# Making the dt columns of a hybrid block by position: 32 weight columns move past tiles of x

## The chip, the cores and the metric

The kernel runs on one core of one Trainium2 chip. The metric is the device time of one execution in microseconds (us), the median of several runs.

## The reference, cut to what matters

A hybrid block works on 256 positions of 2048 channels: a mixer (SSD scan and short convolution), cross attention, a SwiGLU layer, and then a second block of another kind. All is float32. This case is about 32 of the input projection's columns, `dt_raw`, and what is made of them for the scan:

```python
proj = h @ w_in                                   # h: rmsnorm(x), 256 x 2048
z, xbc, dt_raw, sc_u, sc_b, sc_c = jnp.split(proj, IN_SPLITS, axis=-1)   # dt_raw: 256 x 32
dt = jax.nn.softplus(dt_raw + dt_bias)            # 32 heads
a = -jnp.exp(a_log)
...
x = xh * dt[..., None]
a_cs = jnp.cumsum(dt * a, axis=position)          # running sum over the 256 positions
decay = jnp.exp(where(causal, a_cs[..., :, None] - a_cs[..., None, :], -inf))
```

So the scan needs, for each head, dt by position (a column per head, positions on the partitions), and the running sum a_cs in both forms: as rows (heads on the partitions, positions along them) and as columns.

## The kernel before, in words

**Split products.** A float32 product is made of three products in the fp32r format, which TensorE takes in one pass: every weight tile is split into a high part (`wh`, ScalarE, line 1209) and a low part (`wl`, VectorE, line 1556), every activation tile lies in SBUF as 256 high columns and 256 low columns side by side. A tile of 128 x 128 weights is then two matmuls: the high weights stand and 512 columns move past them (line 974), and the low weights stand and 256 columns move (line 971). The result has channels on the partitions. Every matmul has its own weight load (LDWEIGHTS, the rows named PEld).

**Units.** Weights come in units of 512 KB (1024 words in each partition). There are 902 units, in a list built by `columns()`. A unit is loaded by SP (`load`, line 826) into one of four `raw` buffers, split into one of four `wh`/`wl` buffers, and used by TensorE in list order. `schedule()` is an order written out by hand: each step s holds unit s of TensorE and pieces of work for the other engines (`PLAN[s]`); every engine walks through the steps in order and does its own pieces. The split of unit s+3 is a piece of step s, so weights are split three units ahead. The split of unit u on ScalarE waits until TensorE is through unit u-4, and SP's load of unit u waits for the split of unit u-4.

**The dt column.** It comes after `b` 1, as units 24 and 25: `w_dt` is the 32 columns padded with zeros to 128, so that the 16 tiles of 128 x 128 take two units of eight tiles, all into bank 0 (`ONE`, line 964), 32 of 128 output partitions in use. Unit 26 begins the column `u` 2, and `c` 2 is the next to write bank 0. Pieces `dt0` to `dt6` follow at 2, 7, 8, 12, 14, 18 and 19 steps behind unit 25:

- dt0: ScalarE copies the low half of the sum out of PSUM, VectorE adds the high half, multiplies with the norm's factor (a row, 32 partitions) and adds dt_bias.
- dt1 to dt4: softplus by |x|, exp, ln and a correction step (a reciprocal among it), and then dt*a, on tiles of 32 partitions x 256; the last instruction is the running sum (`tensor_tensor_scan`, line 1793).
- dt5: TensorE turns a_cs and dt into columns, four transposes of 32 x 128 (line 988), and dt6 copies them to `dcol`.
- acsw (16 steps behind): SP writes a_cs to a DRAM scratch, from where it is later broadcast.

**Order of the matmuls.** `unit_orders()` picks, unit by unit, whether 512 and 256 columns alternate (EVEN), come in groups (HEAD), or alternate in twos (TWOS), by where other TensorE work (the set `OTHER`) breaks in.

Of the kernel before, what the change touches and what calls it, by code (L numbers as in the profile page):

```python
# [13 lines left out]
NW = 4  # L14
# [7 lines left out]
    ("hy_b", 18), ("hy_skip", 6), ("norm_ffn_2", 16), ("fc_w", 264), ("fc_b", 88),  # L22
    ("dt_bias", 1), ("a_log", 1), ("f_b1", 1), ("f_fr1", 1), ("f_b2", 1),
    ("f_fr2", 1), ("rcnt", 64),
# [46 lines left out]
def columns():  # L71
# [161 lines left out]
def schedule():  # L233
# [49 lines left out]
    for c in COLS:  # L283
# [197 lines left out]
    for step in at:  # L481
# [4 lines left out]

ONE = [(k, 0, m) for k in range(8) for m in range(2)]
# [4 lines left out]
OTHER = {"nmm", "nmm2", "ntr", "ntr2", "snt", "bmm", "dt5", "cbm", "ssd0", "ssd3", "sn0", "fz1m", "fz2m", "fhm", "fkm", "ztm", "zfm", "zim",  # L492
         "gmm", "pool1", "att0", "att3", "att5", "htr"}


def unit_orders():


    broken = {s + 1: {piece for piece, i in PLAN[s]} & OTHER for s in STEPS if s >= 0}
    starts = sorted({0, *(s for s, other in broken.items() if other and s < NU),  # L500
                     *(u for u in range(1, NU) if UNITS[u - 1][0].src in ("w_o", "w_down_2", "w_gv1") and
                       UNITS[u][0].src != UNITS[u - 1][0].src)})
# [21 lines left out]
def program(nc, T_):  # L524
# [38 lines left out]
    d_part = [sem(f"d_part{i}") for i in range(4)]  # L563
    d_par0, d_par, d_ident, d_mask, d_f1, d_f2, d_b2 = (sem("d_" + n) for n in ("par0", "par", "ident", "mask", "f1", "f2", "b2"))
    d_out = [sem(f"d_out{i}") for i in range(3)]
# [105 lines left out]
    mask = a_(9728, 384)  # L671
    dtb = [a_(10112 + 256 * i, 256, 32) for i in range(8)]
    acs = dtb[7]
    dcol = a_(12160, 128)
# [221 lines left out]
    def tensor(e):  # L896
# [5 lines left out]
        def unit(u, tiles=range(8), halves_=(0, 1)):  # L902
# [3 lines left out]
            elif u == c.first and c.before:  # L906
# [5 lines left out]
                elif p.kind == "dt":  # L912
                    w.wait_ge(dtV, 1)
                elif p.kind in ("r", "rn"):
# [7 lines left out]
            if u > 1:  # L922
                w.wait_ge(lo, halves(u))
            st, sp = u == c.first, u == c.last
            if c.kind == "v" or c.src == "w_gv1":
                for kk in range(c.kn):
# [35 lines left out]
            else:  # L962
                order = ONE if c.w == 128 else ORDER[u]
                for kk, i, low in order:
                    X, kx, s, n = xtile(c, g * c.kn + kk)
# [24 lines left out]
        for s in STEPS:  # L990
# [15 lines left out]
            for piece, i in PLAN[s]:  # L1006
# [52 lines left out]
                if piece == "dt5":  # L1059
                    w.wait_ge(d_ident, 16)  # L1060
                    w.wait_ge(dtV, 13)
                    for n, src in enumerate((acs, dtb[4])):
                        for st in range(2):
                            o = 64 * n + 32 * st
                            t = turn(banks[7][:, o:o + 32], src[:, 128 * st:128 * st + 128], p=32)
                    t.then_inc(dtP, 1)
                if piece == "cbm":
                    b = banks[4 + i]
                    w.wait_ge(xbc, 4 + i + 1)
                    w.wait_ge(br, 6 * 7 + 1)  # L1070
                    w.wait_ge(dtA, 6)
                    w.wait_ge(nrs, 2)
# [132 lines left out]
    def scalar(e):  # L1205
# [10 lines left out]
        for s in STEPS:  # L1216
            for piece, i in PLAN[s]:
# [3 lines left out]
                if piece == "split":  # L1221
                    r, b = i % NRAW, i % NW
                    w.wait_ge(d_raw[r], 16 * (i // NRAW + (r > 0)))
                    if i >= NW:
                        w.wait_ge(mm, i - NW + 1)
                    copy(wh[:, b * UN:(b + 1) * UN], raw[:, r * UN:(r + 1) * UN]).then_inc(hi, 1)
                if piece == "mgain":
# [160 lines left out]
                if piece == "dt0":  # L1388
                    w.wait_ge(mm, i.last + 1)
                    copy(dtb[1], bank(i, 0)[0:32, 256:512]).then_inc(dtA, 1)  # L1390
                if piece == "dt1":
                    w.wait_ge(dtV, 3)
                    e.activation(dtb[1], dtb[0], ACT.Abs).then_inc(dtA, 1)
                    w.wait_ge(dtA, 2)
                    e.activation(dtb[1], dtb[1], ACT.Exp, scale=-1.0).then_inc(dtA, 1)
                    e.activation(dtb[5][:, 0:1], P("a_log", p=32), ACT.Exp).then_inc(dtA, 1)
# [3 lines left out]
                if piece == "dt6":  # L1400
                    w.wait_ge(dtP, 1)
                    copy(dcol, banks[7][:, 0:128]).then_inc(dtA, 1)
                if piece == "silu":
# [16 lines left out]
                if piece == "ssd1":  # L1420
                    q = i % 2
                    w.wait_ge(d_bb[i % 3], 16 * (i // 3 + 1))
                    w.wait_ge(dtA, 6)
                    if i > 1:
                        w.wait_ge(sMg, i - 1)
                        w.wait_ge(sMv, i - 1)
                    else:
                        w.wait_ge(dtP, 1)
                        w.wait_ge(bsl, 16)
# [122 lines left out]
    def vector(e):  # L1552
# [11 lines left out]
        for s in STEPS:  # L1564
            for piece, i in PLAN[s]:
# [4 lines left out]
                if piece == "split":  # L1570
                    r, b = i % NRAW, i % NW
                    w.wait_ge(hi, halves(i))
                    tt(wl[:, b * UN:(b + 1) * UN], raw[:, r * UN:(r + 1) * UN], wh[:, b * UN:(b + 1) * UN].bitcast(F32),
                       ALU.subtract).then_inc(lo, 1)
# [186 lines left out]
                if piece == "dt0":  # L1761
                    x = dtb[0]
                    w.wait_ge(dtA, 1)
                    tt(x, bank(i, 0)[0:32, 0:256], dtb[1], ALU.add).then_inc(dtV, 1)
                    w.wait_ge(nrs, 1)
                    w.wait_ge(dtV, 1)
                    tt(x, x, rsb(0)[0:32, :], ALU.mult).then_inc(dtV, 1)
                    w.wait_ge(dtV, 2)
                    ts(x, x, P("dt_bias", p=32), None, ALU.add).then_inc(dtV, 1)
                if piece == "dt2":  # L1770
                    w.wait_ge(dtA, 3)
                    ts(dtb[2], dtb[1], 1.0, None, ALU.add).then_inc(dtV, 1)
# [9 lines left out]
                if piece == "dt4":  # L1782
                    b2, b3, b4 = dtb[2], dtb[3], dtb[4]
                    w.wait_ge(dtA, 5)
# [3 lines left out]
                    stt(b4, dtb[0], 0.0, b4, ALU.max, ALU.add).then_inc(dtV, 1)  # L1788
                    w.wait_ge(dtV, 10)
                    ts(b2, b4, dtb[5][:, 0:1], -1.0, ALU.mult, ALU.mult).then_inc(dtV, 1)  # L1790
                    e.memset(b3, 1.0).then_inc(dtV, 1)
# [6 lines left out]
                if piece == "ssd1":  # L1798
                    q = i % 2
                    w.wait_ge(sT, i + 1)  # L1800
                    w.wait_ge(dtA, 6)
                    if i > 1:
                        w.wait_ge(sY, i - 1)
                    else:
                        w.wait_ge(cb, 4)
                        w.wait_ge(dtP, 1)
                    for st in range(2):
# [497 lines left out]
```

## Time and profile before

| | us |
|---|---|
| median of 3 runs | 2587.53 (2586.18 to 2587.93) |
| the profiled execution, first to last instruction (span) | 2585.8 |
| TensorE matmul busy | 2576.9 |
| TensorE weight load busy | 2245.3 |
| VectorE busy | 1893.6 |
| ScalarE busy | 1469.0 |
| GpSimd busy | 316.3 |

The page gives the profiled execution's span and no device time of its own; the median of the runs lies 1.7 us above that span. Busy times overlap: a weight load runs beside the matmul before it. In the rows, PE is TensorE's matmuls, PEld its weight loads, DVE VectorE, ACT ScalarE, POOL GpSimd, and L974 is line 974 of the kernel.

### The profile page before, as it was taken

The page shows a single profiled execution, that of the slowest core. Times are in us where ns is not written, and L with a number is a line of the kernel's source. Part 1 is how long each engine was busy: PE and PEld are TensorE (multiplying, and loading weights), DVE is VectorE, ACT ScalarE, POOL GpSimd, SP SyncE. Part 2 cuts the span into 40 slices and gives each one's busy share as a digit, 9 for nine tenths or more (in the row PEclk, how much of TensorE's full clock was granted, in tenths as well). Part 3 has the DMA queues.
Part 4 walks back from the last instruction along what each step waited for, and adds up shares of the span by engine and source line. Part 5 has one row for each costly group of instructions (what it writes and reads, how often), then busy time and mean ns, then how long its engine had stood idle before and what let it go on. Part 6 is the DMA issues. An engine that isn't in the chain of part 4 may idle for free.

```text
span 2585.8 us, 37666 instructions
## 1 busy us (share of the span) xinstructions
PE 2576.9 (100%) x14704; PEld 2245.3 (87%) x14704; DVE 1893.6 (73%) x2859; ACT 1469.0 (57%) x2244; POOL 316.3 (12%) x292
## 2 busy tenths in 40 slices
PE   9999999999999999999999999999999999999998
PEld 8888888888899888888888888888888888888887
DVE  7787777777977866666666698788876766667675
ACT  6666657776656444444444466445654545555554
POOL 2111103316201010101000043101100000000000
PEclk9999999999999999999999999999999999999999
DMA  7665666666656656666666666556666666666665
GB/s 245 181 221 186 188 200 199 175 207 189 211 172 197 182 173 189 190 192 187 192 189 190 192 184 224 157 171 189 187 198 192 190 193 189 194 189 194 188 190 159
DMA packets 137065, 493.73 MB, mean 191 GB/s; under 512 B 15415, under 2 KB 15800, under 8 KB 136504
## 3 DMA queue, kind: packets, MB, share of 16 engines
q1 hardware_dynamic: 136456, 490.80, 62.7%
q8 instruction: 116, 1.90, 0.3%
q14 instruction: 61, 0.50, 0.1%
q10 hardware_dynamic: 432, 0.53, 0.1%
HBM read 489.14 MB, written 2.13 MB: 190 GB/s over the span
## 4 chain that ended last, share of the span: by engine, by line
PE 99%; DMA 0%; ACT 0%; DVE 0%; issue 0%; SPq 0%; ACTq 0%
PE ps L974 56%; PE ps L971 28%; PE ps L947 3%; PE ps L946 3%; PE ps L948 3%; PE ps L935 0%; PE ps L936 0%; PE ps L934 0%; PE ps L988 0%; PE ps L1097 0%; PE ps L960 0%; PE ps L959 0%; PE ps L961 0%; PE ps L1184 0%; PE ps L1173 0%; PE ps L1153 0%
## 5 line engine op out<-in xcount | busy, mean ns | idle before, releaser
L974 PE MATMUL ps<-X,wh 128*128 128x512 f32 x4752 | 1591.1, 395 | 1.1 <-DVE X L1562 1.1
L1556 DVE TENSOR_TENSOR wl<-raw,wh 128x1024 fp32r<-128x1024 f32 (+1 forms) x908 | 1149.7, 1269 | 511.8 <-ACT wh L1209 511.1
L1209 ACT ACTIVATE wh<-raw 128x1024 fp32r<-128x1024 f32 (+1 forms) x908 | 955.4, 1055 | 730.8 <-PE ps L971 555.1
L971 PE MATMUL ps<-X,wl 128*128 128x256 f32 x4752 | 1199.0, 278 | 0.0
L974 PEld LDWEIGHTS ps<-X,wh 128*128 128x128 f32 x4752 | 862.8, 188 | 171.9 <-issue 3.0
L971 PEld LDWEIGHTS ps<-X,wl 128*128 128x128 f32 x4752 | 872.0, 188 | 37.9
L974 PE MATMUL ps<-XG,wh 128*128 128x512 f32 x1472 | 492.0, 394 | 0.0
L971 PE MATMUL ps<-XG,wl 128*128 128x256 f32 x1472 | 371.6, 278 | 0.0
L974 PEld LDWEIGHTS ps<-XG,wh 128*128 128x128 f32 x1472 | 266.8, 188 | 53.1 <-issue 0.9
L1209 ACT ACTIVATE T<-ps 128x256 f32<-128x256 f32 x444 | 145.7, 380 | 251.5 <-PE ps L971 249.7
L971 PEld LDWEIGHTS ps<-XG,wl 128*128 128x128 f32 x1472 | 269.7, 188 | 11.3
L2108 POOL TENSOR_TENSOR hT<-hT,T 128x256 f32<-128x256 f32 x144 | 123.3, 877 | 820.1 <-DVE hT L1556 820.0
L1556 DVE TENSOR_TENSOR hT<-hT,ps 128x256 f32<-128x256 f32 (+1 forms) x280 | 109.3, 437 | 52.5 <-ACT T L1209 44.4
L946 PE MATMUL ps<-wh,XG 128*128 128x512 f32 x352 | 137.0, 389 | 0.0
L947 PE MATMUL ps<-wl,XG 128*128 128x512 f32 x352 | 136.9, 389 | 0.0
L948 PE MATMUL ps<-wh,XG 128*128 128x512 f32 x352 | 136.9, 389 | 0.0
L1562 DVE SCALAR_TENSOR_TENSOR T<-R,par,T 128x256 f32<-128x256 f32 x260 | 109.0, 482 | 0.8 <-ACT T L1366 0.8
L2108 POOL TENSOR_TENSOR T<-T 128x512 f32<-128x512 f32 (+1 forms) x54 | 71.4, 1326 | 231.2 <-ACT T L1267 216.8
L1556 DVE TENSOR_TENSOR T<-ps,T 128x256 f32<-128x256 f32 x130 | 49.0, 418 | 48.7 <-ACT T L1209 48.6
L1556 DVE TENSOR_TENSOR R<-ps,T 128x256 f32<-128x256 f32 x130 | 49.0, 419 | 48.3 <-ACT T L1209 48.3
L946 PEld LDWEIGHTS ps<-wh,XG 128*128 128x128 f32 x352 | 66.1, 188 | 13.8
L948 PEld LDWEIGHTS ps<-wh,XG 128*128 128x128 f32 x352 | 66.1, 188 | 13.7
(228 smaller groups left out, 1629.6 us busy)
## 6 DMA issues: line engine op xcount, KB each, us to landing
raw<-in_w_gate SPq DMA_DIRECT2D x176, 512.0 KB, 3.7
raw<-in_w_down SPq DMA_DIRECT2D x176, 512.0 KB, 3.7
raw<-in_w_sc SPq DMA_DIRECT2D x95, 512.0 KB, 4.1
raw<-in_w_up SPq DMA_DIRECT2D x88, 512.0 KB, 3.8
raw<-in_w_val SPq DMA_DIRECT2D x88, 512.0 KB, 3.6
raw<-in_w_zx SPq DMA_DIRECT2D x80, 512.0 KB, 4.1
raw<-in_w_in SPq DMA_DIRECT2D x56, 512.0 KB, 3.9
raw<-in_w_osc SPq DMA_DIRECT2D x32, 512.0 KB, 3.7
```

What stands on the lines that cost most here:

```text
L946: e.matmul(bank(c, i)[:, :], xh, wh[:, b0:b0 + 512], start=not goes and st and kk == 0, stop=False)
L947: e.matmul(bank(c, i)[:, :], xh, wl[:, b0:b0 + 512], start=False, stop=False)
L948: t = e.matmul(bank(c, i)[:, :], xl, wh[:, b0:b0 + 512], start=False, stop=sp and kk == c.kn - 1 and (not goes or c.kind == "on"))
L971: t = e.matmul(bank(c, i)[:, 0:256], wl[:, b0:b0 + 128], X[:, kx * 512:kx * 512 + 256], start=False, stop=sp and kk == c.kn - 1)
L974: e.matmul(bank(c, i)[:, :], wh[:, b0:b0 + 128], X[:, kx * 512:kx * 512 + 512], start=st and kk == 0, stop=False)
L1209: return e.activation(out, in_, ACT.Copy, scale=scale)
L1556: return e.tensor_tensor(out, a, b, op)
L1562: return e.scalar_tensor_tensor(out, a, s1, b, op0, op1)
L2108: return e.tensor_tensor(out, a, b, op)
```

## The change

`w_dt` is no longer padded: 32 columns x 16 tiles are one unit of 256 KB, so there are 901 units. The roles in the matmul are swapped. The activation tiles stand and the weights move: for each of 16 channel tiles and each of the two halves of the positions, the high activations (128 channels x 128 positions) stand while 64 columns move (32 high weights, 32 low weights side by side), and then the low activations stand while the 32 high weights move. The result has positions on the partitions: 128 x 64 in each of banks 0 and 1. Softplus and dt*a then run on tiles of 128 x 64, dt lands in `dcol` directly, and dt_bias and a_log come by a DMA that broadcasts 128 values to all partitions. dt*a is turned into rows (dt5, two transposes of 128 x 32), the running sum is made from PSUM (dt6), and a_cs is turned back into columns (dt7, two transposes of 32 x 128) and copied (dt8). The pieces stand at 1, 3, 4, 5, 7, 18, 20, 30 and 31 steps behind the dt unit, acsw at 21.

```diff
-            add("dt", 0, "w_dt", 0, range(2), "1", 0, w=128, kn=8)
+            add("dt", 0, "w_dt", 0, range(1), "1", 0, w=32, kn=16)
...
-            for n, d in enumerate((2, 7, 8, 12, 14, 18, 19)):
+            for n, d in enumerate((1, 3, 4, 5, 7, 18, 20, 30, 31)):
                 put(e + d, "dt%d" % n, c)
-            put(e + 16, "acsw", 0)
+            put(e + 21, "acsw", 0)
...
+    def by_tile(t, b):
+        return t[:, b * UN:b * UN + 1024].rearrange("p (k m) -> p k m", k=16)
...
-            e.dma_start(raw[:, r * UN:(r + 1) * UN], T_[col.src][col.c, g]).then_inc(d_raw[r], 16)
+            n = col.w * col.kn
+            e.dma_start(raw[:, r * UN:r * UN + n], T_[col.src][col.c, g]).then_inc(d_raw[r], 16)
...
+                        e.dma_start(dtp, T_["dtp"].to_broadcast([128, 128])).then_inc(d_dtp, 16)
...
+            if c.kind == "dt":
+                both = by_tile(wh, u % NW)
+                for kk in range(16):
+                    X, kx, s, n = xtile(c, kk)
+                    w.wait_ge(s, n)
+                    for i in range(2):
+                        xh, xl = (X[:, kx * 512 + o + 128 * i:kx * 512 + o + 128 * i + 128] for o in (0, 256))
+                        e.matmul(bank(c, i)[:, 0:64], xh, both[:, kk, :], start=kk == 0, stop=False)
+                        t = e.matmul(bank(c, i)[:, 0:32], xl, both[:, kk, 0:32], start=False, stop=kk == 15)
+                t.then_inc(mm, 1)
+                return
...
                 if piece == "dt5":
                     w.wait_ge(d_ident, 16)
+                    w.wait_ge(dtV, 11)
+                    for st in range(2):
+                        t = turn(banks[7][0:32, 128 * st:128 * st + 128], dtb[2][:, 32 * st:32 * st + 32])
+                    t.then_inc(dtP, 1)
+                if piece == "dt7":
                     w.wait_ge(dtV, 13)
-                    for n, src in enumerate((acs, dtb[4])):
-                        for st in range(2):
-                            o = 64 * n + 32 * st
-                            t = turn(banks[7][:, o:o + 32], src[:, 128 * st:128 * st + 128], p=32)
+                    for st in range(2):
+                        t = turn(banks[7][:, 256 + 32 * st:288 + 32 * st], acs[:, 128 * st:128 * st + 128], p=32)
                     t.then_inc(dtP, 1)
...
-                    copy(dtb[1], bank(i, 0)[0:32, 256:512]).then_inc(dtA, 1)
+                    w.wait_ge(nv, 5)
+                    for st in range(2):
+                        copy(dtb[1][:, 32 * st:32 * st + 32], bank(i, st)[:, 32:64], col_of(0, 4 + st, 1)).then_inc(dtA, 1)
...
+                if piece == "dt6":
+                    w.wait_ge(dtP, 1)
                     w.wait_ge(dtV, 12)
-                    e.tensor_tensor_scan(acs, b3, b2, 0.0, ALU.mult, ALU.add).then_inc(dtV, 1)
+                    e.tensor_tensor_scan(acs, dtrow, banks[7][0:32, 0:256], 0.0, ALU.mult, ALU.add).then_inc(dtV, 1)
...
-    arr["w_dt"] = pack(wd, 128, 8)
+    arr["w_dt"] = pack(w_in[:, 5120:5152], 32, 16)
+    arr["dtp"] = np.concatenate([I["dt_bias"][0]] * 2 + [I["a_log"][0]] * 2).reshape(1, 128)
```

## Rows read from the trace of the kernel before

**Rows 1.** The page: busy times, granted clock in 40 slices, chain that ended last, costliest group.

```profile
PE 2576.9 (100%) x14704; PEld 2245.3 (87%) x14704; DVE 1893.6 (73%) x2859; ACT 1469.0 (57%) x2244; POOL 316.3 (12%) x292
...
PEclk9999999999999999999999999999999999999999
...
PE 99%; DMA 0%; ACT 0%; DVE 0%; issue 0%; SPq 0%; ACTq 0%
...
L974 PE MATMUL ps<-X,wh 128*128 128x512 f32 x4752 | 1591.1, 395 | 1.1 <-DVE X L1562 1.1
```

**Rows 2.** Timeline of PE, end of b 1 to u 2: start, duration (us), instruction.

```profile
76.40 0.40 PE L974 MATMUL ps<-X,wh 128*128 128x512 f32 x1
...
81.83 0.28 PE L971 MATMUL ps<-X,wl 128*128 128x256 f32 x1
81.94 0.46 PE L974 MATMUL ps<-X,wh 128*128 128x512 f32 x1
```

**Rows 3.** Timeline of PEld, the weight loads of eight matmuls of one column.

```profile
629.30 0.98 PEld L1106 LDWEIGHTS ps<-ones,T 128*128 128x128 f32 x8
630.19 0.30 PEld L974 LDWEIGHTS ps<-XG,wh 128*128 128x128 f32 x2
```

**Rows 4.** Groups of weight loads by shape: busy us, mean ns of one.

```profile
L974 PEld LDWEIGHTS ps<-X,wh 128*128 128x128 f32 x4752 | 862.8, 188 | 171.9 <-issue 3.0
L900 PEld LDWEIGHTS ps<-ones 128*128 128x128 f32 x18 | 3.9, 331 | 1.0 <-POOL ones L2104 1.0
L1106 PEld LDWEIGHTS ps<-ones,T 128*128 128x128 f32 x16 | 2.0, 190 | 0.1
L988 PEld LDWEIGHTS ps<-ident,A 32*128 32x128 f32 x4 | 0.3, 138 | 0.2 <-issue 0.2
```

**Rows 5.** Timeline of PE, matmuls of 256 moving columns only (the values' column).

```profile
756.21 0.28 PE L934 MATMUL ps<-wh,XM 128*128 128x256 f32 x1
...
756.57 0.28 PE L934 MATMUL ps<-wh,XM 128*128 128x256 f32 x1
```

**Rows 6.** Timeline of PE, the transposes of dt5.

```profile
132.33 0.27 PE L971 MATMUL ps<-X,wl 128*128 128x256 f32 x1
132.53 0.43 PE L988 MATMUL ps<-ident,A 32*128 32x32 f32 x4
132.90 0.50 PE L1057 MATMUL ps<-XM 128*128 128x512 f32 x1
```

**Rows 7.** Timeline of PE, two transposes of full tiles between two units.

```profile
45.02 0.28 PE L971 MATMUL ps<-X,wl 128*128 128x256 f32 x1
45.14 0.38 PE L988 MATMUL ps<-ident,T 128*128 128x128 f32 x2
...
45.83 0.40 PE L971 MATMUL ps<-X,wl 128*128 128x256 f32 x2
```

**Rows 8.** Timeline of VectorE and of PE around unit 43.

```profile
127.86 2.32 DVE L1556 TENSOR_TENSOR wl<-raw,wh 128x1024 fp32r<-128x1024 f32 x2
...
129.67 0.40 PE L974 MATMUL ps<-X,wh 128*128 128x512 f32 x1
```

**Rows 9.** Timeline of SP's queue, the parameters at the start.

```profile
18.68 0.47 SPq L851 DMA_DIRECT2D A<-in_mask  x1
```

**Rows 10.** Timeline of PE at the start of the kernel.

```profile
0.99 4.21 PE L900 MATMUL ps<-ones 128*128 128x128 f32 x18 [0.99 <-POOL ones L2104]
6.33 0.76 PE L974 MATMUL ps<-X,wh 128*128 128x512 f32 x1 [1.13 <-DVE X L1562]
...
7.11 0.63 PE L974 MATMUL ps<-X,wh 128*128 128x512 f32 x1
...
7.75 0.63 PE L974 MATMUL ps<-X,wh 128*128 128x512 f32 x1
...
10.47 0.40 PE L974 MATMUL ps<-X,wh 128*128 128x512 f32 x1
...
10.82 0.39 PE L974 MATMUL ps<-X,wh 128*128 128x512 f32 x1
```

More of the change, by code:

```diff
@@ L22 @@
     ("hy_b", 18), ("hy_skip", 6), ("norm_ffn_2", 16), ("fc_w", 264), ("fc_b", 88),
-    ("dt_bias", 1), ("a_log", 1), ("f_b1", 1), ("f_fr1", 1), ("f_b2", 1),
+    ("f_b1", 1), ("f_fr1", 1), ("f_b2", 1),
     ("f_fr2", 1), ("rcnt", 64),
@@ L483, in schedule @@
     return at
-ONE = [(k, 0, m) for k in range(8) for m in range(2)]
 EVEN = [(k, i, m) for k in range(4) for i in range(2) for m in range(2)]
@@ L491 @@
 TWOS = [(k, i, m) for k in range(4) for m in range(2) for i in range(2)]
-OTHER = {"nmm", "nmm2", "ntr", "ntr2", "snt", "bmm", "dt5", "cbm", "ssd0", "ssd3", "sn0", "fz1m", "fz2m", "fhm", "fkm", "ztm", "zfm", "zim",
+OTHER = {"nmm", "nmm2", "ntr", "ntr2", "snt", "bmm", "dt5", "dt7", "cbm", "ssd0", "ssd3", "sn0", "fz1m", "fz2m", "fhm", "fkm", "ztm", "zfm", "zim",
          "gmm", "pool1", "att0", "att3", "att5", "htr"}
@@ L500, in unit_orders @@
     starts = sorted({0, *(s for s, other in broken.items() if other and s < NU),
-                     *(u for u in range(1, NU) if UNITS[u - 1][0].src in ("w_o", "w_down_2", "w_gv1") and
+                     *(u for u in range(1, NU) if UNITS[u - 1][0].src in ("w_dt", "w_o", "w_down_2", "w_gv1") and
                        UNITS[u][0].src != UNITS[u - 1][0].src)})
@@ L563, in program @@
     d_part = [sem(f"d_part{i}") for i in range(4)]
-    d_par0, d_par, d_ident, d_mask, d_f1, d_f2, d_b2 = (sem("d_" + n) for n in ("par0", "par", "ident", "mask", "f1", "f2", "b2"))
+    d_par0, d_par, d_ident, d_mask, d_dtp, d_f1, d_f2, d_b2 = (sem("d_" + n) for n in (
+        "par0", "par", "ident", "mask", "dtp", "f1", "f2", "b2"))
     d_out = [sem(f"d_out{i}") for i in range(3)]
@@ L671, in program @@
     mask = a_(9728, 384)
-    dtb = [a_(10112 + 256 * i, 256, 32) for i in range(8)]
-    acs = dtb[7]
+    dtb = [a_(10112 + 64 * i, 64) for i in range(7)]
+    dtp = a_(10624, 128)
+    dtrow, acs = a_(10880, 256, 32), a_(11904, 256, 32)
     dcol = a_(12160, 128)
@@ L912, in unit @@
                 elif p.kind == "dt":
-                    w.wait_ge(dtV, 1)
+                    w.wait_ge(dtV, 2)
                 elif p.kind in ("r", "rn"):
@@ L962, in unit @@
             else:
-                order = ONE if c.w == 128 else ORDER[u]
-                for kk, i, low in order:
+                for kk, i, low in ORDER[u]:
                     X, kx, s, n = xtile(c, g * c.kn + kk)
@@ L1070, in tensor @@
                     w.wait_ge(br, 6 * 7 + 1)
-                    w.wait_ge(dtA, 6)
+                    w.wait_ge(dtA, 7)
                     w.wait_ge(nrs, 2)
@@ L1225, in scalar @@
                         w.wait_ge(mm, i - NW + 1)
+                    if UNITS[i][0].kind == "dt":
+                        copy(by_tile(wh, b)[:, :, 0:32], raw[:, r * UN:r * UN + 512].rearrange("p (k m) -> p k m", k=16)).then_inc(hi, 1)
+                        continue
                     copy(wh[:, b * UN:(b + 1) * UN], raw[:, r * UN:(r + 1) * UN]).then_inc(hi, 1)
@@ L1393, in scalar @@
                     e.activation(dtb[1], dtb[0], ACT.Abs).then_inc(dtA, 1)
-                    w.wait_ge(dtA, 2)
+                    w.wait_ge(dtA, 3)
                     e.activation(dtb[1], dtb[1], ACT.Exp, scale=-1.0).then_inc(dtA, 1)
-                    e.activation(dtb[5][:, 0:1], P("a_log", p=32), ACT.Exp).then_inc(dtA, 1)
+                    w.wait_ge(d_dtp, 16)
+                    e.activation(dtb[5], dtp[:, 64:128], ACT.Exp).then_inc(dtA, 1)
                 if piece == "dt3":
@@ L1399, in scalar @@
                     e.activation(dtb[3], dtb[2], ACT.Ln).then_inc(dtA, 1)
-                if piece == "dt6":
-                    w.wait_ge(dtP, 1)
-                    copy(dcol, banks[7][:, 0:128]).then_inc(dtA, 1)
+                if piece == "dt8":
+                    w.wait_ge(dtP, 2)
+                    copy(dcol[:, 0:64], banks[7][:, 256:320]).then_inc(dtA, 1)
                 if piece == "silu":
@@ L1422, in scalar @@
                     w.wait_ge(d_bb[i % 3], 16 * (i // 3 + 1))
-                    w.wait_ge(dtA, 6)
+                    w.wait_ge(dtA, 7)
                     if i > 1:
@@ L1427, in scalar @@
                     else:
-                        w.wait_ge(dtP, 1)
+                        w.wait_ge(dtP, 2)
                         w.wait_ge(bsl, 16)
@@ L1572, in vector @@
                     w.wait_ge(hi, halves(i))
+                    if UNITS[i][0].kind == "dt":
+                        both = by_tile(wh, b)
+                        tt(both[:, :, 32:64], raw[:, r * UN:r * UN + 512].rearrange("p (k m) -> p k m", k=16),
+                           both[:, :, 0:32].bitcast(F32), ALU.subtract).then_inc(lo, 1)
+                        continue
                     tt(wl[:, b * UN:(b + 1) * UN], raw[:, r * UN:(r + 1) * UN], wh[:, b * UN:(b + 1) * UN].bitcast(F32),
@@ L1761, in vector @@
                 if piece == "dt0":
[L1762 to L1767, printed above, removed]
+                    for st in range(2):
+                        q = slice(32 * st, 32 * st + 32)
+                        w.wait_ge(dtA, st + 1)
+                        stt(dtb[0][:, q], bank(i, st)[:, 0:32], col_of(0, 4 + st, 1), dtb[1][:, q], ALU.mult, ALU.add).then_inc(dtV, 1)
+                    w.wait_ge(d_dtp, 16)
                     w.wait_ge(dtV, 2)
-                    ts(x, x, P("dt_bias", p=32), None, ALU.add).then_inc(dtV, 1)
+                    tt(dtb[0], dtb[0], dtp[:, 0:64], ALU.add).then_inc(dtV, 1)
                 if piece == "dt2":
-                    w.wait_ge(dtA, 3)
+                    w.wait_ge(dtA, 4)
                     ts(dtb[2], dtb[1], 1.0, None, ALU.add).then_inc(dtV, 1)
@@ L1783, in vector @@
                     b2, b3, b4 = dtb[2], dtb[3], dtb[4]
-                    w.wait_ge(dtA, 5)
+                    w.wait_ge(dtA, 6)
                     w.wait_ge(dtV, 8)
@@ L1787, in vector @@
                     w.wait_ge(dtV, 9)
-                    stt(b4, dtb[0], 0.0, b4, ALU.max, ALU.add).then_inc(dtV, 1)
+                    stt(dcol[:, 64:128], dtb[0], 0.0, b4, ALU.max, ALU.add).then_inc(dtV, 1)
                     w.wait_ge(dtV, 10)
-                    ts(b2, b4, dtb[5][:, 0:1], -1.0, ALU.mult, ALU.mult).then_inc(dtV, 1)
-                    e.memset(b3, 1.0).then_inc(dtV, 1)
+                    stt(b2, dcol[:, 64:128], -1.0, dtb[5], ALU.mult, ALU.mult).then_inc(dtV, 1)
+                    e.memset(dtrow, 1.0).then_inc(dtV, 1)
+                if piece == "dt6":
+                    w.wait_ge(dtP, 1)
                     w.wait_ge(dtV, 12)
-                    e.tensor_tensor_scan(acs, b3, b2, 0.0, ALU.mult, ALU.add).then_inc(dtV, 1)
+                    e.tensor_tensor_scan(acs, dtrow, banks[7][0:32, 0:256], 0.0, ALU.mult, ALU.add).then_inc(dtV, 1)
                 if piece == "cbv":
@@ L1800, in vector @@
                     w.wait_ge(sT, i + 1)
-                    w.wait_ge(dtA, 6)
+                    w.wait_ge(dtA, 7)
                     if i > 1:
@@ L1805, in vector @@
                         w.wait_ge(cb, 4)
-                        w.wait_ge(dtP, 1)
+                        w.wait_ge(dtP, 2)
                     for st in range(2):
@@ L2263 @@
         "hy_skip": cols(I["hy_skip_2"][0]), "norm_ffn_2": cols(I["norm_ffn_2"][0]), "fc_w": taps(I["ffn_conv_w_2"][0]),
-        "fc_b": cols(I["ffn_conv_b_2"][0]), "dt_bias": pad(I["dt_bias"][0]),
-        "a_log": pad(I["a_log"][0]), "f_b1": pad(I["hy_filt_b1_2"][0]), "f_fr1": pad(I["hy_filt_freq1_2"][0]),
+        "fc_b": cols(I["ffn_conv_b_2"][0]), "f_b1": pad(I["hy_filt_b1_2"][0]), "f_fr1": pad(I["hy_filt_freq1_2"][0]),
         "f_b2": pad(np.tile(I["hy_filt_b2_2"][0], 2)), "f_fr2": pad(np.tile(I["hy_filt_freq2_2"][0], 2)),
```

2 lines of the change are left out of this document (removed).

## The prediction, made before the changed kernel had run

> **What bounds the kernel now.** Read the page first: TensorE's matmuls are busy all through the span, the granted clock is at its upper level (2.4 GHz) in all 40 slices, and the chain that ended last is TensorE for 99% [rows 1]. The costliest group shows 1.1 us of idle time ahead of 4752 matmuls [rows 1]. Nothing that another engine does faster can be won back, since TensorE waits for nobody; the time is the sum of what its instructions take. So the view to read is TensorE's timeline, start to start, since the durations in it overlap. Where 512 and 256 moving columns alternate, a pair takes 0.35 us from start to start (the last two rows of [rows 10]); where only 256 columns move, three matmuls take 0.36 us, 0.120 each [rows 5].
>
> The profiled execution has a span of 2585.8 us; the median of the runs, 2587.5, lies 1.7 above it. I add the sum of the changes to the median.
>
> **The dt matmuls, removed.** Two units of 8 pairs, 32 matmuls, from 76.40 to 81.94: 5.54 us [rows 2]. All on the path.
>
> **The dt matmuls, added.** 16 channel tiles x 2 halves of the positions x 2 (high and low activations) = 64 matmuls, every one with its own load of 128 x 128 standing values, with 64 and 32 columns moving in turn. By columns alone they are little: 32 x 96 = 3072 columns against 16 x 768 = 12288 before, a quarter. But the count of weight loads doubles from 32 to 64, and for so few columns the load should be what paces them. No fp32r matmul of under 256 columns is in this trace, so I bound its price.
> - The nearest row has the same standing size and less to move: eight matmuls of one column (float32). Their loads start at 629.30, the next instruction's at 630.19: 0.89 us for 8, 0.111 each [rows 3]. One load is recorded as 190 ns there and as 188 ns for the fp32r tiles [rows 4], so the two load alike.
> - Above: at 256 columns per load the pace is 0.120 [rows 5]. If load and stream did not overlap at all, it would be 0.111 plus the stream; at 0.120 per 256 columns the mean of 48 columns adds 0.023, which gives 0.134.
> - Below: the four transposes with 32 standing rows take 0.43 us together, one alone 0.23 or so, so 0.07 each [rows 6]; their load is recorded as 138 ns [rows 4].
>
> I take 0.114, near the one-column row and a little towards the 256-column one: 64 x 0.114 = 7.3 us. Ends: 64 x 0.07 = 4.5 and 64 x 0.134 = 8.6. Against the 5.54 removed: **+1.8 us** (-1.0 to +3.1).
>
> The Trainium skill, page "TensorE: Matmul & The Clock Gate", section "Back-to-back issue gap", gives about 81 ns per matmul for a stream of loads and matmuls of 128 columns; by it the 64 would take 5.2 us and the whole be 0.4 us shorter rather than 1.8 longer. The trace's own loads of 4-byte tiles came every 111 ns [rows 3], so I don't use it.
>
> **The transposes.** Before: four of 32 x 128 in one break. From the last matmul of the unit to the next work 0.57 us (132.33 to 132.90) where 0.12 is usual, and 0.11 more on the matmul behind (0.50 instead of 0.39): 0.56 us [rows 6]. After: dt7 has two of these, 0.56 less two at 0.07, so 0.43. dt5 has two with 32 standing columns and 128 moving. Two transposes of full tiles cost 0.23: 45.02 to 45.83 is 0.81, where one short and two long matmuls take 0.58 [rows 7]; if the change of the array's shape costs dt5 what it costs dt7, it is 0.43. I take 0.33. Sum 0.76 against 0.56: **+0.2 us** (+0.1 to +0.3). By the hand-written order both fall behind units that `bmm` already breaks, so no further unit is reordered but the one behind dt.
>
> **The unit less, and the feed.** One split on ScalarE and VectorE goes, the other is half as long, and SP loads 256 KB instead of 1 MB. None of it is on the path. While TensorE spends 7.3 us in one unit, the splits of the next three units are done, and the split of unit 28 waits for the end of the dt unit as every split waits for the unit four back. So the feed behind dt is no tighter than elsewhere. Cost 0; without that cover it would be one split, 1 to 2 us.
>
> **Softplus on 128 x 64 instead of 32 x 256.** The same dozen small instructions with a quarter of the columns. VectorE's tightest place was here: behind the old scan, two splits (127.86, 1.16 each) end at 129.0 and 130.2, and unit 43 starts at 129.67 [rows 8], 0.6 us of slack. With dt4 eight steps earlier relative to it and shorter, the slack grows. But slack that was never used up pays nothing: 0. The pieces are now crowded into steps 25 to 31; each adds under 1.5 us to a step of 2.77. ScalarE's wait for `dtV` 3 in dt1 has the splits of later units queued behind it; VectorE has made dt0 two steps earlier. dt6's wait on TensorE's transposes, and SP's wait in acsw, are passed likewise: VectorE reaches its step only after the later split it does first, which itself waits for a later unit of TensorE. 0.
>
> **The DMA of dt_bias and a_log.** One more issue behind the mask (0.47 us there [rows 9]) puts the following weight loads back by about half a microsecond at 19 us, and they have over a microsecond in hand. 0; 0.5 if not.
>
> **Sum.** +1.8 + 0.2 = +2.0: **2589.5 us**, that is 0.08% slower and within what a measurement of this kernel can tell from no change (0.2%, 5.2 us). The likeliest case's own range is 2588 to 2591.
>
> **Rivals.**
> - *The clock falls in the dt unit (slower).* For 7.3 us TensorE would be issuing without a gap, yet move columns for only a sixth to a fifth of the time (3072 columns; at 0.120 per 256 that is 1.4 us). If the chip takes that for idleness, the granted clock drops to 1.2 GHz inside the unit. Against: in the row of one-column matmuls it stayed up, but that lasted under 1 us [rows 3, 1]; nothing in the trace has such a stretch of 7 us. For: at the start, the 18 matmuls of the warm-up kept TensorE busy from 0.99 to 5.2 us and the pairs still ran at half speed until about 10 us: 0.64 us from 7.11 to 7.75, against 0.35 from 10.47 to 10.82 [rows 10]; a load at that level took 331 ns, not 190 [rows 4]. Price: from the fall on, the rest of the unit takes twice its time (3.6 us more if it falls halfway), and then some 4 us pass at half speed before it is back, as from 6.33 to 10.4 [rows 10], which loses 4 x (1 - 0.35/0.64) = 1.8. Together +5.4, so **2595**; a late fall gives 2591.5, an early one 2597.5. It decides slower as soon as the fall comes with more than 1.4 us of the unit's work still to do.
>  The Trainium skill's page "TensorE: Matmul & The Clock Gate", Part 1 and Part 4, says that the gate follows how busy the array is, and that transposes do not count as busy in the same way though they are issued; by it a stretch of issue with little computing could lose the clock. No row here shows this.
> - *Loads are hidden better than I think.* At 0.07 the unit takes 4.5 us: -1.0 + 0.2, **2586.7**. For: transposes reach it [rows 6]. Against: their load is recorded 50 ns shorter than the fp32r one [rows 4].
> - *A narrow fp32r matmul is taken in two passes*, as float32 ones are here (nine warm-up matmuls in the code are 18 records [rows 10]): 128 loads at 0.111 are 14.2 us, +8.7 + 0.2, **2596.4**. Against: no fp32r matmul in the trace is doubled.
> - *The lighter vector work shows (faster).* It would need a TensorE that waits now; its idle time of 1.1 us in the main group [rows 1] is at the start. At most 1 us, no verdict.
>
> **Chances.** Forecast 0.50; the clock falls 0.30; cheaper loads 0.08; two passes 0.06; something in the moved pieces that I missed, either way, 0.06. Slower by over 0.2% means above 2592.7: three quarters of the clock case (0.22) and the two passes (0.06), 0.28. Faster by over 0.2% comes from no case that I can price, 0.03. The rest, 0.69, is within 0.2%. The range has to hold the forecast, the cheaper loads and most of the clock case: 2585.5 to 2597.
>
> **What would show it.** TensorE's timeline: the dt unit's 64 matmuls, 32 with 64 and 32 with 32 columns, in 7.3 us; 0.111 to 0.120 from start to start shows the load as the pace, 0.07 the second rival, 0.2 and more from some point on the first, together with a granted clock under 1 in that slice and pairs of 0.64 behind it. 128 records instead of 64 would be the third. The gap at each of dt5 and dt7 should be 0.2 to 0.45 us. The group of main matmuls should show as little idle time as now; the sum of matmul starts outside these places should not move. I am wrong if a wait appears on a split between 85 and 110 us, where the small pieces are crowded now, or if the unit's loads cost over 0.15 each at full clock.

## The result, and the profile after

| | before | after |
|---|---|---|
| median | 2587.34 us (2586.06 to 2588.34, 10 runs) | 2592.76 us (2591.22 to 2595.61, 10 runs) |
| profiled execution, span | 2585.8 us | 2589.4 us |
| mean granted clock of the ten runs | | 0.996 to 0.998 |

The ratio is 1.0022, 95% interval 1.0014 to 1.0030: slower by 5.4 us. It lies inside the range, but not where the likeliest case put it (2588 to 2591). The profiled execution (2591.22) was the shortest of the ten, so what follows explains the cheap end.

The page looks as before: every one of the 40 slices has the clock digit 9, and the main group has 1.6 us of idle time, at the start, against 1.1 [rows 1]. A slice is 65 us long; what happened took 7.

```profile
PE 2580.0 (100%) x14736; PEld 2249.4 (87%) x14736; DVE 1890.0 (73%) x2858; ACT 1467.8 (57%) x2244; POOL 312.0 (12%) x292
...
PEclk9999999999999999999999999999999999999999
...
L991 PE MATMUL ps<-X,wh 128*128 128x512 f32 x4736 | 1584.5, 395 | 1.6 <-DVE X L1588 1.6
```

The timeline of PE over the dt unit (start, duration, instruction) answers to [rows 2]. Lines 939 and 940 are the narrow matmuls.

```profile
74.95 0.27 PE L988 MATMUL ps<-X,wl 128*128 128x256 f32 x1
75.07 0.19 PE L939 MATMUL ps<-wh,X 128*128 128x64 f32 x1
...
79.90 0.28 PE L939 MATMUL ps<-wh,X 128*128 128x64 f32 x1
80.01 0.35 PE L940 MATMUL ps<-wh,X 128*128 128x32 f32 x1
80.20 0.40 PE L939 MATMUL ps<-wh,X 128*128 128x64 f32 x1
80.41 0.37 PE L940 MATMUL ps<-wh,X 128*128 128x32 f32 x1
...
83.82 0.37 PE L940 MATMUL ps<-wh,X 128*128 128x32 f32 x1
84.04 2.05 PE L991 MATMUL ps<-X,wh 128*128 128x512 f32 x4
85.89 1.05 PE L988 MATMUL ps<-X,wl 128*128 128x256 f32 x4
86.74 0.69 PE L991 MATMUL ps<-X,wh 128*128 128x512 f32 x2
```

Read the starts. Up to 80.01 they are 0.11 us apart (but for the very first pair), with 64 and with 32 columns alike; from 80.20 they are 0.21 apart; unit 25 then starts at half speed too (four matmuls in 85.89 - 84.04 = 1.85 us, where a 512-column one takes 0.23 otherwise) and is back at its pace from 86.74. The windows show the clock beside it (columns: busy time and count of each engine, PEclk, DMA share, GB/s):

```profile
74.00:78.00 4.00, 4.00 (x36) 3.87 (x34) 3.93 (x8) 1.83 (x4) 0.00 (x0) 1.00 0.52 154
78.00:82.00 4.00, 4.00 (x30) 4.00 (x29) 3.86 (x8) 0.00 (x0) 0.00 (x0) 0.76 0.29 113
82.00:86.00 4.00, 4.00 (x16) 3.61 (x16) 0.62 (x1) 1.71 (x4) 0.00 (x0) 0.50 0.42 131
86.00:90.00 4.00, 4.00 (x24) 3.62 (x23) 2.61 (x7) 1.85 (x4) 1.44 (x2) 0.89 0.47 131
90.00:94.00 4.00, 4.00 (x25) 3.51 (x25) 2.45 (x3) 2.29 (x6) 0.00 (x0) 1.00 0.47 131
```

TensorE is busy for all of the 4.00 us in each and never waits; the granted clock fell to 0.50 (1.2 GHz) just after 80 us, some 5 us into the unit, and was back 6.8 us later. Nothing else moved: behind unit 25 the matmuls keep their distance from those of the kernel before, within 0.3 us and without drift, and at the end of the span only the 0.1 of the two transposes below has been added.

The sum, start to start: 64 matmuls at 0.1115 are 7.14, less 5.54: **+1.6**. The 18 at half clock cost 0.102 more each: **+1.8**. Unit 25 took 4.16 us (84.04 to 88.20), where the same column's first unit took 2.84 before: **+1.3**. The transposes: **+0.1** (below). Together, before rounding, +4.9. The start-up differs from one execution to the next: in the kernel before, the pairs reached full speed only at 10.4 us [rows 10], here at 6.7. To compare executions without it, I use the time from the last matmul start of `b` 1 (74.95 here, 76.28 before) to the end of the span: 2514.4 against 2509.5, +4.9. I call this the tail. A tail is one execution, a median is all of them; the medians keep the start-up in.

The two places with transposes, in the same timeline, answer to [rows 6, 7]:

```profile
135.75 0.28 PE L988 MATMUL ps<-X,wl 128*128 128x256 f32 x1
135.86 0.38 PE L1005 MATMUL ps<-ident,A 128*32 128x128 f32 x2
136.00 0.48 PE L1074 MATMUL ps<-XM 128*128 128x512 f32 x1
...
169.79 0.27 PE L988 MATMUL ps<-X,wl 128*128 128x256 f32 x1
169.99 0.31 PE L1005 MATMUL ps<-ident,A 32*128 32x32 f32 x2
170.23 0.50 PE L1074 MATMUL ps<-XM 128*128 128x512 f32 x1
```

The unit with `bmm` and dt5 takes 3.48 us and the one with `bmm` and dt7 3.68, where `bmm` alone makes 3.25: 0.24 + 0.43 = 0.67 against 0.56.

### The profile page after: what moved, and what is told of

It is laid out like the page before. It is cut to its first block, busy times and chain, and to the rows that moved or that the text cites. A ratio compares the mean times of both kernels' runs of the same rounds, so it can differ in the third digit from the quotient of the medians.

```text
span 2589.4 us, 37730 instructions
## 1 busy us (share of the span) xinstructions
PE 2580.0 (100%) x14736; PEld 2249.4 (87%) x14736; DVE 1890.0 (73%) x2858; ACT 1467.8 (57%) x2244; POOL 312.0 (12%) x292
## 4 chain that ended last, share of the span: by engine, by line
PE 99%; DMA 0%; ACT 0%; DVE 0%; issue 0%; SPq 0%; ACTq 0%
PE ps L991 56%; PE ps L988 28%; PE ps L966 3%; PE ps L964 3%; PE ps L965 3%; PE ps L953 0%; PE ps L954 0%; PE ps L952 0%; PE ps L1005 0%; PE ps L1117 0%; PE ps L978 0%; PE ps L979 0%; PE ps L977 0%; PE ps L1204 0%; PE ps L1193 0%; PE ps L1173 0%
## 5 line engine op out<-in xcount | busy, mean ns | idle before, releaser
L1229 ACT ACTIVATE wh<-raw 128x1024 fp32r<-128x1024 f32 (+2 forms) x907 | 954.3, 1054 | 742.3 <-PE ps L988 565.5
```

What stands on the lines that cost most here:

```text
L1229: return e.activation(out, in_, ACT.Copy, scale=scale)
```

## The experiments

Theory A: with few columns moving per weight load, the granted clock is lowered, though TensorE issues without a gap. Its main rivals: the 64 loads themselves or the many short instructions do it; or something beside the unit (a bank, the crowded pieces).

**wide256.** The same 64 loads, with 256 columns behind each instead of 64 or 32.

```diff
-e.matmul(bank(c, i)[:, 0:64], xh, both[:, kk, :], start=kk == 0, stop=False)
-t = e.matmul(bank(c, i)[:, 0:32], xl, both[:, kk, 0:32], start=False, stop=kk == 15)
+out = bank(c, i)[:, 0:256].rearrange("p (r m) -> p r m", r=4)
+mv = both[:, kk, :].unsqueeze(1).to_broadcast([128, 4, 64])
+e.matmul(out, xh, mv, start=kk == 0, stop=False)
+t = e.matmul(out, xl, mv, start=False, stop=kk == 15)
```

> The changed kernel, but each of the dt unit's 64 matmuls moves the same 64 weight columns four times over, so 256 columns instead of 64 or 32 (the copies land in unused columns of the bank; nothing reads them). 64 loads as before. Theory A (the clock falls because the dt unit moves few columns for 9 us): the granted clock stays up, the unit takes 64 x 0.120 = 7.7 us, and the kernel is 2.3 us slower than the kernel before: about 2589.6, faster than the changed kernel although it moves over five times the columns. Rival B (the clock falls because of the standing activations, the doubled loads, or the place in the kernel, whatever moves): it falls again, and the kernel is at 2593 or more. Rival C (no part of the loss is the clock; it is the moved pieces): 2593.3, 0.5 above the changed kernel.

2590.01 us (2588.57 to 2590.63, 11 runs), ratio 1.0012 [1.0003, 1.0021]. Timeline of PE at the unit's ends, then the windows over it:

```profile
75.14 0.28 PE L941 MATMUL ps<-wh,X 128*128 128x256 f32 x1
...
82.69 0.28 PE L942 MATMUL ps<-wh,X 128*128 128x256 f32 x1
82.81 0.63 PE L993 MATMUL ps<-X,wh 128*128 128x512 f32 x2
```

```profile
74.00:78.00 4.00, 4.00 (x32) 3.87 (x31) 3.93 (x8) 1.90 (x4) 0.00 (x0) 1.00 0.54 153
78.00:82.00 4.00, 4.00 (x36) 4.00 (x35) 3.93 (x8) 0.00 (x0) 0.00 (x0) 1.00 0.28 110
82.00:86.00 4.00, 4.00 (x28) 3.60 (x27) 1.83 (x4) 2.15 (x6) 0.00 (x0) 1.00 0.45 135
```

More columns and less time: every matmul costs 0.120 instead of 0.111, the unit 7.67 instead of 8.97, and the clock stays at 1.00 over the unit and behind it; the tail is +2.2 instead of +4.9. All eleven runs have a mean clock of 0.999 or 1.000. So neither the count of loads nor the crowded pieces lower the clock. What differs is how many columns move (and are written) behind each load.

**twice.** The narrow stretch made longer.

```diff
-                for kk in range(16):
+                for kk in [k for k in range(16)] * 2:
```

> The changed kernel with the dt unit's 64 matmuls issued twice (dt_raw doubles, so the outputs differ). Theory A: the clock stays down as long as the narrow stretch lasts, so the second 64 take 0.2135 each where the first ones fell to, 13.7 us, and the time is 2592.8 + 13.7 = about 2606.5. If the fall lasts for a fixed time only and then the clock comes back while narrow matmuls go on, the second 64 cost between 7.1 and 11 us: 2600 to 2604. Without any clock effect on them: 2592.8 + 7.1 = 2599.9.

2607.52 us (2604.64 to 2609.34, 4 runs), ratio 1.0080 [1.0067, 1.0094], a microsecond above what A gave. The windows of its trace:

```profile
76.00:80.00 4.00, 4.00 (x35) 3.96 (x33) 3.90 (x7) 1.60 (x3) 0.00 (x0) 0.89 0.67 222
80.00:90.00 10.00, 10.00 (x48) 10.00 (x49) 3.02 (x7) 0.00 (x0) 0.00 (x0) 0.50 0.21 67
90.00:100.00 10.00, 10.00 (x48) 10.00 (x49) 0.00 (x0) 0.00 (x0) 0.00 (x0) 0.50 0.00 0
```

The stretch begins at 76.19. The clock goes down once, at 79.1, which is 2.9 us into it and earlier than the 5.0 of the changed kernel, and it stays down as long as narrow matmuls go on: 48 in 10 us, 0.21 each. It is back at 106.4, 5.7 us behind the last of them.

**mix.** 16 matmuls of unit 25, one ahead of every four narrow ones, so that more columns move in the same stretch.

```diff
+                w.wait_ge(evD, EVN[UNITS[u + 1][0].before.n])
+                w.wait_ge(lo, halves(u + 1))
...
                 for kk in range(16):
+                    one(u + 1, *EVEN[kk])
...
-                t.then_inc(mm, 1)
+                t.then_inc(mm, 2)
```

> The changed kernel, with the 16 matmuls of unit 25 put among the dt unit's, one ahead of each four narrow ones. Same matmuls, same loads, another order. Theory A: the columns moved in the same time more than double (3072 and 6144 in about 9.9 us); if that is enough the granted clock stays up, and the time is the kernel before plus 1.6 (64 loads at 0.1115 less 5.54) and 0.1 for the transposes, about 2589.1; if it isn't enough, the clock falls somewhat later or for less time, 2590 to 2593. Rival B (narrow matmuls or their loads as such bring it down): as slow as the changed kernel or slower, since the slow stretch now holds wide matmuls too: 2593 to 2596.

2605.66 us (2604.82 to 2606.18, 5 runs), ratio 1.0074 [1.0061, 1.0087]: a miss for both, and a fault of the experiment. The timeline of PE shows it:

```profile
76.50 0.27 PE L1004 MATMUL ps<-X,wl 128*128 128x256 f32 x1
81.88 0.77 PE L917 MATMUL ps<-X,wh 128*128 128x512 f32 x1 [5.11 <-DVE T L1598]
```

The column of unit 25 may be written only when VectorE has emptied the bank of `b` 1. The dt units had always covered that; here TensorE idled for 5.11 us, and the clock fell as it resumed. It stayed down for 23.9 us, through the mixed block and 5 us past it, and the tail is +18.3. Less the wait and the 1.7 of the sum at full clock, 11.5 us are left; what of them comes from idling and what from the mixture can't be told apart here.

**fold.** The kernel before with its dt matmuls packed otherwise: high and low weights stand side by side (64 columns), 512 columns move once, 16 matmuls in all.

```diff
+                for kk in range(16):
+                    t = e.matmul(bank(c, 0)[0:64, :], both[:, kk, :], X[:, kx * 512:kx * 512 + 512], start=kk == 0, stop=kk == 15)
...
-                    copy(dtb[1], bank(i, 0)[0:32, 256:512]).then_inc(dtA, 1)
+                    copy(dtb[1], bank(i, 0)[0:32, 256:512])
+                    copy(dtb[2], bank(i, 0)[32:64, 0:256]).then_inc(dtA, 1)
```

> The kernel before with only the packing of the weights changed: the 32 high and 32 low weight columns of a tile stand side by side (64 standing columns) and the 512 columns of x move past them once: 16 matmuls of 512 columns give all products (high x high, high x low, low x high, and the tiny low x low, which nothing reads). One unit less. Softplus by heads as in the kernel before, with one more small add. Expected: 5.54 us removed, 16 x 0.227 = 3.6 added, 0.2 for the change of the array's shape at both ends, so -1.7: 2585.6, clock at its upper level throughout. Rival: standing columns under 128 make every matmul in the row pay a drain (0.2 us instead of 0.117 was seen once ahead of such a tile); then 16 x 0.09 more, and no gain: 2587.

2588.60 us (2587.50 to 2589.83, 11 runs), ratio 1.0007 [0.9998, 1.0016]: the gain didn't come. Timeline of PE:

```profile
79.76 2.00 PE L936 MATMUL ps<-X,wh 128*64 128x512 f32 x8
83.00 0.50 PE L987 MATMUL ps<-X,wh 128*128 128x512 f32 x1 [1.24 <-DVE T L1573]
```

The dt unit would have taken 3.67 us (16 x 0.229) instead of 5.54. Unit 25 began 5.08 us after it (77.92 to 83.00) instead: 1.4 us went into a wait for the same bank. Two waits of 0.4 followed later, and the tail is +0.7. The dt units of the kernel before were just long enough to cover that bank.

**free.** The changed kernel with dt in a bank of its own and the later columns numbered as if dt weren't there, so that unit 25 writes a bank that was emptied long ago. It is the base for the next two.

```diff
+        col.q = sum(d.kind != "dt" for d in cols) % 2
+        if pair is None:
+            col.pair = col.q
...
-            add("dt", 0, "w_dt", 0, range(1), "1", 0, w=32, kn=16)
+            add("dt", 0, "w_dt", 0, range(1), "1", 0, w=32, kn=16, pair=3)
...
-        return tile(2 * (c.n % 2) + i, n)
+        return tile(2 * (c.q) + i, n)
```

> The changed kernel with the dt unit's sums in banks 6 and 7 instead of 0 and 1, and the columns behind it numbered as if dt were not there, so that unit 25 no longer needs the bank that b 1 leaves. Nothing else moves: a control for the three others. Theory A (narrow columns cost the clock): as the changed kernel, 5 to 6 us above the kernel before, clock down for 7 us or more from some point in the dt unit. If banks or the wait for b 1 had a share in the loss, it would be nearer to 2 us.

2594.93 us (2591.24 to 2596.16, 8 runs), ratio 1.0028 [1.0018, 1.0039]; its before 2586.70 (28 runs). That is +8.2 where 5 to 6 were expected. Windows of the profiled execution, the longest of the eight:

```profile
78.00:82.00 4.00, 4.00 (x34) 4.00 (x34) 3.90 (x7) 1.26 (x3) 0.00 (x0) 0.89 0.64 224
82.00:86.00 4.00, 4.00 (x21) 4.00 (x20) 2.28 (x5) 0.00 (x0) 0.00 (x0) 0.50 0.33 100
86.00:90.00 4.00, 4.00 (x16) 3.61 (x16) 1.06 (x1) 2.02 (x5) 0.00 (x0) 0.50 0.09 35
90.00:94.00 4.00, 4.00 (x22) 3.51 (x21) 2.17 (x7) 1.54 (x2) 1.44 (x2) 0.83 0.45 131
```

The dt unit begins at 77.46; the clock is down from 81.2, 3.7 us into it, for 10.2 us. The dt unit takes 10.1 us, unit 25 4.6, and the tail is +7.5. Of that, 1.0 has nothing to do with dt: transposes at 1580.33 wait 0.73 us for ScalarE, which no other trace here shows. The clock falls without the bank or the wait for `b` 1, so they have no part in the fall.

**parts.** The same 64 narrow matmuls on `free`, in stretches of 20, 24 and 20 with whole units between.

```diff
+            if u == DT - 1:
+                part(range(0, 5))
...
+            if u == DT - 1:
+                part(range(5, 11))
...
+            if u == DT + 1:
+                part(range(11, 16)).then_inc(mm, 2)
```

> As the control, with the dt unit's 64 matmuls cut into three stretches of 20, 24 and 20 (2.2, 2.7 and 2.2 us) that stand ahead of unit 23, behind it and behind unit 25, so that a full unit of 2.77 us lies between. Theory A: if what counts is how long little is moved at a stretch, the granted clock stays up, and the time is 1.6 (64 x 0.1115 less 5.54) and 0.1 for the transposes above the kernel before: 1.7, about 2588.3. If the mean over a longer time counts, it falls all the same, and it is 3 to 8 us above. Rival (loads of activations as such): falls, as the control.

2590.30 us (2588.17 to 2591.74, 11 runs), ratio 1.0015 [1.0006, 1.0024], 4.6 us under `free`. Windows over the stretches:

```profile
74.00:78.00 4.00, 4.00 (x33) 3.79 (x32) 2.73 (x6) 2.98 (x5) 0.00 (x0) 1.00 0.31 89
78.00:82.00 4.00, 4.00 (x33) 3.74 (x31) 3.90 (x7) 1.60 (x3) 0.00 (x0) 1.00 0.71 226
82.00:86.00 4.00, 4.00 (x29) 3.62 (x28) 2.65 (x6) 0.00 (x0) 0.00 (x0) 1.00 0.22 68
86.00:90.00 4.00, 4.00 (x31) 3.72 (x31) 0.91 (x1) 2.00 (x6) 0.00 (x0) 1.00 0.21 84
```

The clock stays at 1.00, and every narrow matmul takes 0.111. Measured from the last matmul of unit 22, since the first stretch lies ahead of unit 23, the rest of the execution is 1.9 us longer than before's, where +1.7 was the sum without a fall. The median is 2.0 above the expected 2588.3, but all eleven runs have a mean clock of 0.999 or 1.000. Same instructions, another order: the fall needs more of them in a row. The margin is thin: the longest stretch here took 2.6 us, and in `twice` the clock fell after 2.9. What length is safe, no run shows.

**mix2.** `mix` again, on `free`, where the bank is ready.

> As the control, with the 16 matmuls of unit 25 put one ahead of each four narrow ones, this time with its bank free from the start (the first attempt began with a wait of 5.1 us, which took the clock down before the mixture had started, so it said nothing on it). About 40% of the mixed stretch of 9.9 us moves columns, against 18% in the dt unit alone. Theory A: the clock stays up and the kernel is 1.7 us above the kernel before, or, if that share isn't enough, it falls during the stretch: then 10 us or more above, since at the lower level the mixture did not get it back for 20 us in the first attempt. Nothing in between is expected but by chance of where it falls.

2592.57 us (2589.05 to 2598.45, 8 runs), ratio 1.0023 [1.0013, 1.0033]. No wait ahead of the block this time, and still the clock fell, near its end. Windows:

```profile
80.00:84.00 4.00, 4.00 (x35) 3.85 (x34) 3.43 (x8) 0.00 (x0) 0.00 (x0) 1.00 0.28 94
84.00:88.00 4.00, 4.00 (x26) 3.70 (x27) 0.04 (x1) 1.13 (x2) 0.00 (x0) 0.82 0.34 120
88.00:92.00 4.00, 4.00 (x20) 3.45 (x19) 3.90 (x7) 2.33 (x6) 1.45 (x2) 0.76 0.42 111
```

It fell at 86.5, as the block ended, for 3.4 us; the tail is +3.3, between the two outcomes that were expected. The runs spread over 9.4 us (mean clock 0.999 in the shortest, 0.996 in the longest), so this pattern sometimes costs little and sometimes much. A mixture is not enough; whole units between the stretches of `parts` were.

**fold2.** `fold` with the banks of `free` and the softplus pieces at 2, 3, 4, 8, 12, 18 and 19 steps behind, to see whether the gain of 1.9 us is there without the wait.

```diff
-            for n, d in enumerate((2, 7, 8, 12, 14, 18, 19)):
+            for n, d in enumerate((2, 3, 4, 8, 12, 18, 19)):
```

> The folded form (64 standing weight columns, 512 moving columns of x, 16 matmuls) with its sum in bank 6, so that unit 25 need not wait for b 1's bank (that wait was 1.7 us in the first folded kernel, whose unit was 2 us shorter), and with the softplus pieces at 2, 3, 4, 8 and 12 steps, away from the step that held up unit 40 and 42 by 0.4 us each. Expected: the 1.9 us of shorter matmuls now show: 2585.5 against a kernel before at 2587.3, or 1.5 to 2.0 below it; clock at its upper level. If it is level with the kernel before, the wait has only moved on.

2587.26 us (2585.72 to 2587.91, 11 runs), ratio 1.0001 [0.9992, 1.0010]; tail -0.2. The wait at the bank is gone, and a new one is there, in PE's timeline and, ahead of it, in VectorE's:

```profile
114.16 0.27 PE L988 MATMUL ps<-X,wl 128*128 128x256 f32 x1
115.05 0.47 PE L991 MATMUL ps<-X,wh 128*128 128x512 f32 x1 [0.62 <-DVE wl L1577]
```

```profile
103.81 1.23 DVE L1577 TENSOR_TENSOR wl<-raw,wh 128x1024 fp32r<-128x1024 f32 x1 [3.61 <-ACT wh L1226]
104.95 0.28 DVE L1580 TENSOR_SCALAR A<-A 32x256 f32<-32x256 f32 x1
105.26 0.41 DVE L1577 TENSOR_TENSOR A<-A 32x256 f32<-32x256 f32 x1
105.61 1.73 DVE L1807 RECIPROCAL A<-A 32x256 f32<-32x256 f32 x1
```

**fold3.** `fold2` with that step one unit earlier, into VectorE's idle time ahead of 103.81.

```diff
-            for n, d in enumerate((2, 3, 4, 8, 12, 18, 19)):
+            for n, d in enumerate((2, 3, 4, 7, 12, 18, 19)):
```

> fold2 with the fourth softplus step (the 1.73 us reciprocal of 32x256 and its neighbours) one unit earlier, in VectorE's idle time of 3.61 us ahead of 103.81. In fold2 it ran from 104.95, and the waits of 0.78 us at 115.05 and 0.47 us at 123.94 followed, both ended by the split of weights on VectorE. Theory (the gain of folding is 1.9 us on TensorE and VectorE's lateness takes it back): both waits go or shrink below 0.3 us in sum, dt unit 3.55 us, clock up throughout, 2586.0 us, 1.2 us under fold2, ratio to before about 0.9995. Rival (the lateness comes from the order of the splits and ScalarE's share, not from the reciprocal): the waits stay within 0.3 us of their size and the time is 2587.2 us.

2586.86 us (2585.06 to 2588.76, 11 runs) against 2586.78 (15 runs), ratio 1.0000 [0.9990, 1.0009]. The wait of 0.78 us went, the other stayed at 0.45, the tail is -1.1. Half the theory: the reciprocal caused the first wait and not the second. The median shows nothing of it; a microsecond is too little for these runs.

## Why the prediction was right or wrong

**The likeliest case was wrong, the first rival was what happened.** The range holds the time only because that rival had been priced. The failed step is its weighing: 0.50 for a unit at full clock throughout, against 0.30 for a fall. In the changed kernel's profile, in `free`, and in the unit doubled, the clock fell each time that 64 or more narrow matmuls came in a row, 5.0, 3.7 and 2.9 us into them. None of the ten runs of the changed kernel had a mean clock above 0.998, where those of `wide256` have 0.999 to 1.000, as have 61 of 64 runs of the kernel before taken beside the experiments. What I held against it, that the clock stayed up over the eight one-column matmuls [rows 3], said nothing on seven microseconds: `parts` keeps it up too, with stretches of 20 to 24.

What I held for it, the warm-up [rows 10], didn't speak either. The changed kernel has the same 18 matmuls, and behind them a pair takes 0.35 us at once (7.15 to 7.50), not 0.64:

```profile
0.99 4.15 PE L907 MATMUL ps<-ones 128*128 128x128 f32 x18 [0.99 <-POOL ones L2136]
7.15 0.40 PE L991 MATMUL ps<-X,wh 128*128 128x512 f32 x1
7.50 0.39 PE L991 MATMUL ps<-X,wh 128*128 128x512 f32 x1
```

`twice`, with the same start as the changed kernel, is back at a granted clock of 0.50 from 8 to 10 us. So whether the first pairs run at half speed varies from execution to execution, and that the rival came true is no credit to this row. Nor can the start be read from the page's clock: in the kernel before, the window 8.00:10.00 shows a granted clock of 1.00 while pairs take 0.64 us [rows 10], so "2.4 GHz in all 40 slices" was not true of the pairs before 10.4 us.

The Trainium skill's page "TensorE: Matmul & The Clock Gate", Part 1, has the gate follow how busy the array has been. By the profile's busy time, 4.00 of 4.00 us, TensorE was as busy as it can be when the clock fell, so the trace fits that only if narrow matmuls count for less; what the chip counts, no run here shows. The advice of the Trainium skill's same page, in "Why this matters for your kernels", to leave no long idle gaps would not have warned: there was no gap.

**Its price** was put too high. The prediction has 5.4 us for a fall halfway on top of the +2.0, 2595 in all. (Its 2597.5 for an early fall leaves the first microsecond at full clock; from the start on, its own terms give 2589.5 + 7.3 + 1.8 = 2598.6, above the range.) The measured 5.4 is the whole change; less the 1.7 of the unit at full clock and the transposes, the fall cost 3.7 in the median. That both figures read 5.4 is chance. In the profiled execution the fall came at the 47th matmul, later than halfway, and cost 1.8 in the unit (3.6 was named for halfway) and 1.3 behind it (1.8). The runs that were not profiled are longer, as a rule with a lower mean clock: the six runs with a mean clock of 0.998 took 2591.22 to 2592.86, the three with 0.997 2592.79 to 2594.77, and the one with 0.996 is the longest (2595.61). Why the clock falls earlier or for longer in one run than in another, no run here settles.

**The dt matmuls at full clock** held: 0.1115 each against 0.114, +1.6 against +1.8. The load is the pace, as the row of one-column matmuls said [rows 3]. Neither 0.07 nor two passes showed: 64 records, all at 0.11 until the fall. The 81 ns per matmul of the Trainium skill's page "TensorE: Matmul & The Clock Gate", section "Back-to-back issue gap", is not what this trace shows.

**The transposes** cost +0.11 against +0.2: dt7 0.43 as worked out, dt5 0.24, the price of full-tile transposes [rows 7], so the change of the array's shape that I had added half of isn't charged to 32 standing columns.

**Feed, softplus and the DMA** at nothing: held. No wait between 85 and 110 us, and every unit behind 25 at its old pace. What the lighter vector work freed paid nothing. What I had not seen is that the dt column itself was a cover: unit 26 could not start before `b` 1's bank was empty, which `fold` shows 5.1 us after dt began. It did not touch the changed kernel, whose unit is longer, but it ate the gain of `fold`.

**What a sum without the clock would have given** is measured twice: `wide256` and `parts`, +2.2 and +1.9 in one execution each, without the start-up, which is the forecast of +2.0. Their medians are +3.5 and +3.6 with intervals of about 2.3 either way: they hold +2.0, but only at their ends.

## What to carry to other kernels

Where few columns move past each weight load, price TensorE by its loads (0.111 us each here for 128 x 128 fp32r tiles, whether 32 or 64 columns move, and for float32 tiles with one column), not by its columns; swapping the operands to move 32 columns instead of 512 saves nothing if it doubles the loads. Keep such stretches short and put whole units of wide matmuls between them: the same 64 matmuls cost 1.8 us (the changed kernel, each against its own before) to 4.6 us (`free`) more in one stretch than in three, by the medians. And before shortening a stretch on the bounding engine, find what it covers: here a bank being emptied took back 1.4 of 1.9 us, and then a reciprocal 0.8.

## What the runs showed of the hardware

- The granted clock fell to 1.2 GHz while TensorE issued without a gap, 5.0 us (changed kernel), 3.7 (`free`) and 2.9 (`twice`) into a stretch of narrow matmuls. With 256 columns behind each of the same loads (`wide256`), or in stretches of 2.2 to 2.6 us with whole units between (`parts`), it stayed at 2.4 GHz.
- At 1.2 GHz a narrow matmul with its load takes 0.213 us, against 0.111. In the changed kernel's trace one load is recorded as 333 ns there, against 192 at 2.4 GHz: the load slows with the clock as well.
- How long the clock stayed down varied: 6.8 us (changed kernel), 10.2 (`free`), 3.4 (`mix2`), 27.3 (`twice`) and 23.9 (`mix`, after 5.1 us of idling).
- At 2.4 GHz 256 columns behind a load cost 0.120, 64 columns 0.111: between them moving more is nearly free.
